# First shift vector of the adaptive modulation summed on VectorE, second shift's products placed between mixer tiles, silu after two of four sums of squares

## The chip, the cores and the metric

The kernel runs on one core of a Trainium2 chip. A core has a matrix engine (TensorE, PE in the profile; its weight loads are PEld), VectorE (DVE), ScalarE (ACT), GpSimd (POOL) and SyncE (SP), which here only issues transfers. The metric is the time of one execution in device microseconds, as the median of several runs; lower is better.

## The reference, cut to what matters

Two blocks run one after the other on x (512 tokens of 1024 channels, f32). The change touches only the start of the first block:

```python
def ada_mods(cond, w, b):                       # c: 1x1024, w: 1024x6144
    mods = (jax.nn.silu(cond) @ w + b)[..., None, :]
    return jnp.split(mods, ADA_CHUNKS, axis=-1) # six vectors of 1024

sh1, sc1, g1, sh2, sc2, g2 = ada_mods(c, ada_w[i], ada_b[i])
u = modulate(rms_norm(x, mix_pre_g[i]), sh1, sc1)   # h * (1 + scale) + shift
y = pool_mixer(u, pool_w[j], pool_scale[j])         # (window mean - u) @ w, 4 groups of 256 channels
x = x + g1 * rms_norm(y, mix_post_g[i])
f = conv_ffn(modulate(rms_norm(x, ffn_pre_g[i]), sh2, sc2), ffn_w_up[i], ...)
x = x + g2 * rms_norm(f, ffn_post_g[i])
```

Behind it come the feed-forward part, a gated delta rule mixer and a gated linear attention mixer, each with large f32 products. They make up the span from about 80 us on and are the same in both kernels.

## The kernel before, in words

All six vectors come from one matrix of 24 MB. It is read in 24 units of 1 MB: unit u = 4j + n holds 256 rows of the 1024 columns of vector j (j = 0 first shift, 1 first scale, 2 gate, 3 second shift, 4 second scale, 5 second gate). SP issues them in this order into six slots in SBUF (tile `ada`), each once its slot is free, and puts between them the two halves of the mixer's weights `pool_w` (0.5 MB each) and the first feed-forward weights `raw` (1 MB). The order of the program text is the order on every engine; counters (semaphores) carry the waits.

For vectors 0 to 4 PE multiplies each unit with silu(c) (`ada_unit`, four products of 512 columns on four groups of 32 array columns, line 1787), and counts it in `ada_used`, which frees the slot. After four units VectorE copies the sums to SBUF (`ada_sum`, line 1099), PE adds the four groups and turns the row into columns (`mod_col`, 32 tiny products, line 1797), and VectorE adds the bias (lines 1106 to 1110). The gate takes `mod_row` instead, the second shift's copy is ScalarE's (line 617). Vector 5 is summed by VectorE much later, with one scalar_tensor_tensor per 128 rows (line 1236).

Meanwhile ScalarE normalises x (squares, line 504, root, line 509, scaling, line 573), PE applies the window means in eight `pool_block`s (line 1823), ScalarE copies their results and scales them by 1 + sc1 (line 581), VectorE adds the shift times the sums of the window (line 1150) and scales `pool_w` (line 1138). PE then multiplies each of four token tiles by the mixer weights (`mixed(0)` to `mixed(3)`, eight products each, line 1838). For each tile ScalarE takes squares and root of y, VectorE adds it to x, ScalarE takes squares and root of the new x and scales it to `xn` (lines 504, 509, 597), and PE turns it (`turn_normed`, line 1757), with the units of vectors 3 and 4 between. On ScalarE these steps stand in a fixed order: y0, y1, u0, y2, u1, y3, then the copy of line 617, then u2 and u3. `keep_busy` (line 1763) is PE work without use.

What sets the order around the change is thus the text itself: SP's list of loads, PE's list of units, blocks and tiles, ScalarE's list of squares and scalings.

## Time and profile before

| what | value |
|---|---|
| median of 3 runs | 1144.46 us (1143.86 to 1144.51) |
| profiled execution | 1143.81 us, span 1142.0 us |
| PE / PEld busy | 1125.4 / 920.0 us |
| DVE / ACT / POOL busy | 542.1 / 505.8 / 451.0 us |
| granted PE clock, mean | 0.997 |
| transfers | 128.97 MB, mean 113 GB/s |
| one unit of the adaptive matrix | 1 MB, median 11.3 us from issue to landing |

A time in a row counts from the span's start. Busy PE time includes pipelining, so it is not PE at its peak; what matters for the change is which wait ends last in the first 83 us, since behind that point the work is the same.

### The profile page before, as it was taken

The page shows a single profiled execution, that of the slowest core. Times are in us where ns is not written, and L with a number is a line of the kernel's source. Part 1 is how long each engine was busy: PE and PEld are TensorE (multiplying, and loading weights), DVE is VectorE, ACT ScalarE, POOL GpSimd, SP SyncE. Part 2 cuts the span into 40 slices and gives each one's busy share as a digit, 9 for nine tenths or more (in the row PEclk, how much of TensorE's full clock was granted, in tenths as well). Part 3 has the DMA queues.
Part 4 walks back from the last instruction along what each step waited for, and adds up shares of the span by engine and source line. Part 5 has one row for each costly group of instructions (what it writes and reads, how often), then busy time and mean ns, then how long its engine had stood idle before and what let it go on. Part 6 is the DMA issues. An engine that isn't in the chain of part 4 may idle for free.

```text
span 1142.0 us, 17109 instructions
## 1 busy us (share of the span) xinstructions
PE 1125.4 (99%) x6818; PEld 920.0 (81%) x6818; DVE 542.1 (47%) x878; ACT 505.8 (44%) x701; POOL 451.0 (39%) x342
## 2 busy tenths in 40 slices
PE   9899999999999999999999999999999999999997
PEld 6568888888888888888788878888888888888886
DVE  2472554324452234567986556422200443676825
ACT  4474453544421223875443255754422343534632
POOL 0015544545455371654432211035354444564430
PEclk9999999999999999999999999999999999999999
DMA  8993232232342333434242211122343322223201
GB/s 342 412 376 125 74 110 83 101 110 73 110 128 78 111 111 112 148 106 116 74 114 72 75 38 38 74 74 74 111 124 109 111 79 93 94 75 111 75 1 74
DMA packets 86216, 128.97 MB, mean 113 GB/s; under 512 B 13300, under 2 KB 66306, under 8 KB 85895
## 3 DMA queue, kind: packets, MB, share of 16 engines
q1 hardware_dynamic: 80706, 119.62, 30.8%
q10 hardware_dynamic: 5445, 8.42, 2.2%
q8 instruction: 48, 0.79, 0.3%
q14 instruction: 17, 0.14, 0.0%
HBM read 122.77 MB, written 5.26 MB: 112 GB/s over the span
## 4 chain that ended last, share of the span: by engine, by line
PE 96%; ACT 2%; DVE 2%; issue 1%; POOL 0%; DVEq 0%; ACTq 0%; POOLq 0%
PE ps L292 26%; PE ps L294 25%; PE ps L293 25%; PE ps L1757 3%; PE ps L1787 1%; PE ps L1838 1%; PE ps L2228 1%; PE ps L2229 1%; PE ps L1763 1%; PE ps L2297 1%; PE ps L2287 1%; PE ps L2234 1%; PE ps L1823 1%; PE ps L2052 1%; PE ps L2414 1%; PE ps L2120 1%
## 5 line engine op out<-in xcount | busy, mean ns | idle before, releaser
L429 POOL TENSOR_TENSOR wl<-raw,wh 128x512 fp32r<-128x512 f32 x312 | 420.4, 1379 | 611.6 <-ACT wh L480 611.6
L292 PE MATMUL ps<-xth,wh 128*128 128x512 f32 (+1 forms) x832 | 324.5, 390 | 1.2 <-DVE xtl L1189 0.9
L294 PE MATMUL ps<-xth,wl 128*128 128x512 f32 (+1 forms) x832 | 317.5, 382 | 0.0
L293 PE MATMUL ps<-xtl,wh 128*128 128x512 f32 (+1 forms) x832 | 317.2, 381 | 0.0
L480 ACT ACTIVATE wh<-raw 128x2048 fp32r<-128x2048 f32 x78 | 149.3, 1914 | 305.0 <-PE ps L294 281.3
L292 PEld LDWEIGHTS ps<-xth,wh 128*128 128x128 f32 x832 | 156.5, 188 | 33.8 <-issue 3.7
L294 PEld LDWEIGHTS ps<-xth,wl 128*128 128x128 f32 x832 | 156.4, 188 | 30.6
L293 PEld LDWEIGHTS ps<-xtl,wh 128*128 128x128 f32 x832 | 156.6, 188 | 28.7 <-issue 0.5
L1197 DVE SCALAR_TENSOR_TENSOR conv_out<-ps,conv_taps,conv_out 128x511 f32<-128x511 f32 x44 | 32.7, 744 | 124.8 <-ACT conv_out L650 124.8
L1292 DVE SCALAR_TENSOR_TENSOR conv_v<-ps,gdn_taps,conv_v 128x511 f32<-128x511 f32 (+2 forms) x96 | 71.8, 748 | 40.3 <-ACT conv_v L718 37.4
L292 PE MATMUL ps<-wh,xth 128*128 128x512 f32 x176 | 69.8, 396 | 0.0
L294 PE MATMUL ps<-wh,xtl 128*128 128x512 f32 x176 | 68.6, 390 | 0.0
L293 PE MATMUL ps<-wl,xth 128*128 128x512 f32 x176 | 68.5, 389 | 0.0
L292 PE MATMUL ps<-wh,act_parts_h 128*128 128x512 f32 x160 | 62.4, 390 | 0.0
L293 PE MATMUL ps<-wl,act_parts_h 128*128 128x512 f32 x160 | 62.3, 389 | 0.0
L294 PE MATMUL ps<-wh,act_parts_l 128*128 128x512 f32 x160 | 62.3, 389 | 0.0
L1596 DVE SCALAR_TENSOR_TENSOR xres<-xres,ps 128x1024 f32<-128x1024 f32 x7 | 8.5, 1220 | 90.9 <-PE ps L294 90.9
L718 ACT ACTIVATE conv_v<-ps,gdn_taps 128x512 f32<-128x512 f32 x32 | 21.8, 683 | 55.7 <-PE ps L294 31.0
L292 PE MATMUL ps<-wh,ogt_h 128*128 128x512 f32 x112 | 43.7, 391 | 0.0
L293 PE MATMUL ps<-wl,ogt_h 128*128 128x512 f32 x112 | 43.6, 389 | 0.0
L294 PE MATMUL ps<-wh,ogt_l 128*128 128x512 f32 x112 | 43.6, 389 | 0.0
L1223 DVE CAST act_parts_h<-acts 128x512 fp32r<-128x512 f32 x20 | 9.9, 495 | 65.3 <-PE ps L294 65.3
(349 smaller groups left out, 1634.1 us busy)
## 6 DMA issues: line engine op xcount, KB each, us to landing
ada<-in_ada_w SPq DMA_DIRECT2D x24, 1024.0 KB, 11.3
raw<-in_gdn_w_in SPq DMA_DIRECT2D x24, 1024.0 KB, 5.3
raw<-in_ffn_w_up SPq DMA_DIRECT2D x22, 1024.0 KB, 4.9
raw<-in_gla_w_in SPq DMA_DIRECT2D x12, 1024.0 KB, 5.1
raw<-in_ffn_w_down SPq DMA_DIRECT2D x11, 1024.0 KB, 4.9
raw<-in_gdn_w_out SPq DMA_DIRECT2D x8, 1024.0 KB, 4.9
raw<-in_gla_w_out SPq DMA_DIRECT2D x4, 1024.0 KB, 5.0
xres<-in_x SPq DMA_DIRECT2D x4, 512.0 KB, 5.1
```

The source lines that it names most:

```text
L292: nc.tensor.matmul(o, lh, rh, start=first, stop=False)
L293: nc.tensor.matmul(o, lh, rl, start=False, stop=False)
L294: return nc.tensor.matmul(o, ll, rh, start=False, stop=last)
L429: rest = nc.gpsimd.tensor_tensor(lo[:, part], raw[:, s, part], hi[:, part].bitcast(f32), ALU.subtract)
L480: nc.scalar.activation(wh[:, s if w is None else w, :], raw[:, s, :], ACT.Copy).then_inc(hi_done, 1)
L718: nc.scalar.activation(conv_v[:, sub, :], ps[:, piece_bank(piece), :], ACT.Copy, scale=gdn_taps[:, 3, ch:ch + 1]).then_inc(S("tap3"), 1)
L1197: V.scalar_tensor_tensor(dst[:, 1:T], src[:, 0:T - 1], conv_taps[:, 0, ds(chunk, 1)], dst[:, 1:T], ALU.mult, ALU.add).then_inc(S("conv_lef ...
L1292: V.scalar_tensor_tensor(dst[:, j:T], src[:, 0:T - j], gdn_taps[:, 3 - j, ch:ch + 1], dst[:, j:T], ALU.mult, ALU.add)\
L1757: return X.transpose(o, x, ident[0:n, 0:n])
L1763: X.matmul(ps[:, b, 0:256], ones[:, 0:1].broadcast_to([P, P]), group_rows[:, 0:1].broadcast_to([P, 256]), start=True, stop=True)
L1787: mm = X.matmul(ps[c:c + 32, j % 2, :], c_col[:, k:k + 1].broadcast_to([P, 32]), ada[:, u % ADA_SLOTS, b, half * 512:half * 512 + 512], st ...
L1823: mm = X.matmul(ps[:, 4 + cb % 4, c0:c0 + nc_], xn[:, tt, cb * P:(cb + 1) * P], band_of(cb // 2, tt), start=(tt == 0), stop=(tt == TT - 1) ...
```

## The change

- SP: units 6 to 9 no longer wait for PE's use of units 0 to 3 but for VectorE's sums over them (`shift_summed`). Units 12 and 13 move behind the first feed-forward weights. All units still wait for the fourth tile of x, whose arrival now has a counter of its own (`x_last`).
- VectorE forms the first shift vector: a multiplication and seven scalar_tensor_tensor instructions over 1024 columns into `shift_acc`, behind the window sums. PE's units 0 to 3 and their 32 tiny products go; eight products of `shift_acc` with a column of ones (`shift_col`) come, behind the first scale.
- VectorE scales the first half of `pool_w` before it finishes the scale's column, and the second half in the middle of the shift additions, as before.
- ScalarE: a silu of four columns of ones (a dummy) loads the table. Two sums of squares come before the silu of c, two behind it. The scaling by 1 + sc1 waits for the scale alone.
- PE: `pool_block`s 0 to 3, unit 4, `pool_block`s 4 to 7, units 5 to 7; four `keep_busy` products before unit 8; unit 12 before `mixed(2)` and unit 13 inside it; units 14 and 15 behind `mixed(3)`.

The counts of the semaphores are moved accordingly.

```diff
+                if u >= ADA_SLOTS + 4:
+                    sp.wait_ge(S("ada_used"), u - ADA_SLOTS - 3)
+                elif u >= ADA_SLOTS:
+                    sp.wait_ge(S("shift_summed"), 2 * (u - ADA_SLOTS) + 2)
...
-            sp.wait_ge(S("x_in"), 16 * TT)
+            sp.wait_ge(S("x_last"), 16)
...
-            for u in range(8, 14):
+            for u in range(8, 12):
                 ada_unit(u)
             unit(0, (0, w_up[0, 0]))
-            for u in range(14, 20):
+            for u in range(12, 20):
                 ada_unit(u)
...
-            act.wait_ge(S("rows_turned"), 1)
-            nc.scalar.activation(c_col[:], ps[:, 6, 0:KD], ACT.Silu).then_inc(S("c_silu"), 1)
+            act.wait_ge(S("prepared"), 11)
+            nc.scalar.activation(glast_exp[:, 0, :], ones[:, 0:TT], ACT.Silu)
             for tt in range(TT):
-                act.wait_ge(S("x_in"), 16 * TT)
+                if tt == TT // 2:
+                    act.wait_ge(S("rows_turned"), 1)
+                    nc.scalar.activation(c_col[:], ps[:, 6, 0:KD], ACT.Silu).then_inc(S("c_silu"), 1)
+                act.wait_ge(S("x_in"), 16 * (TT - 1))
+                if tt == TT - 1:
+                    act.wait_ge(S("x_last"), 16)
                 square_sum(junk[:], xres[:, tt, :], stat[:, 0, tt:tt + 1])
...
-            act.wait_ge(S("mods_done"), 2)
+            act.wait_ge(S("mods_done"), 1)
...
+            def shift_sum(k):
+                u = k // 2
+                if k % 2 == 0:
+                    v.wait_ge(ada_full[u], 16)
+                if k == 0:
+                    V.tensor_scalar(shift_acc[:], ada[:, u, 0, :], c_col[:, 0:1], None, ALU.mult).then_inc(S("shift_summed"), 1)
+                else:
+                    v.wait_ge(S("shift_summed"), k)
+                    V.scalar_tensor_tensor(shift_acc[:], ada[:, u, k % 2, :], c_col[:, k:k + 1], shift_acc[:], ALU.mult, ALU.add)\
+                        .then_inc(S("shift_summed"), 1)
...
-            ada_sum(0)
-            mod_col(0, 2, SH1)
...
+            for k in range(KD):
+                shift_sum(k)
             ada_sum(1)
+            scale_weights(0)
             mod_col(1, 3, SC1, PRE1)
+            mod_col(0, 2, SH1)
...
+            def shift_col(b):
+                pe.wait_ge(S("shift_summed"), KD)
+                for k in range(KD):
+                    mm = X.matmul(ps[:, b, k:k + 1], shift_acc[:, k * P:(k + 1) * P], ones[:, 0:1], start=True, stop=True)
+                mm.then_inc(S("mod_mm"), 1)
...
-            ada_unit(0, 0)
-            ada_unit(0, 1)
...
-            ada_unit(0, 2)
-            ada_unit(0, 3)
+            ada_unit(1, 0)
...
-            mod_col(0, 2, 0)
-            mod_col(0, 2, 1)
-            for n in range(4):
+            for n in range(1, 4):
                 ada_unit(1, n)
             mod_col(1, 3, 0)
             mod_col(1, 3, 1)
+            shift_col(2)
+            pe.wait_ge(S("pooled_done"), KD)
+            keep_busy(4, 7)
             ada_unit(2, 0)
-            pe.wait_ge(S("pooled_done"), KD)
...
             mixed(1, gate_row)
-            mixed(2)
+            ada_unit(3, 0)
+            mixed(2, second_shift)
             mixed(3)
-            for n in range(4):
-                ada_unit(3, n)
+            ada_unit(3, 2)
+            ada_unit(3, 3)
             turn_normed(0)
```

PE between the last `pool_block` and the first mixer tile, in the kernel before. Rows of line 1797 are `mod_col`, of 1787 `ada_unit`:

```order
L1797 MATMUL ps<-group_rows,ada_part 32x1 [waits ada_summed]
L1797 MATMUL ps<-group_rows,ada_part 32x1 x15
L1797 MATMUL ps<-group_rows,ada_part 32x1 [waits ada_summed]
L1797 MATMUL ps<-group_rows,ada_part 32x1 x15
L1787 MATMUL ps<-ada,c_col 32x512 [waits ada_full4]
L1787 MATMUL ps<-ada,c_col 32x512 x3
L1787 MATMUL ps<-ada,c_col 32x512 [waits ada_full5]
```

And from units 6 and 7 on in the changed kernel, whose lines 1806, 1816, 1902 and 1783 are `ada_unit`, `mod_col`, `shift_col` and `keep_busy`:

```order
L1806 MATMUL ps<-ada,c_col 32x512 [waits ada_full1]
L1806 MATMUL ps<-ada,c_col 32x512 x3
L1816 MATMUL ps<-group_rows,ada_part 32x1 [waits ada_summed]
L1816 MATMUL ps<-group_rows,ada_part 32x1 x15
L1816 MATMUL ps<-group_rows,ada_part 32x1 [waits ada_summed]
L1816 MATMUL ps<-group_rows,ada_part 32x1 x15
L1902 MATMUL ps<-ones,shift_acc 128x1 [waits shift_summed]
L1902 MATMUL ps<-ones,shift_acc 128x1 x7
L1783 MATMUL ps<-group_rows,ones 128x256 [waits pooled_done]
L1783 MATMUL ps<-group_rows,ones 128x256 x3
L1806 MATMUL ps<-ada,c_col 32x512 [waits ada_full2]
```

The first set of `mod_col` is gone, and eight full-width products and four of `keep_busy` stand between the scale's column and unit 8.

VectorE over the same stretch, before (line 1086 is the window sums, 1138 the scaling of `pool_w`):

```order
L1086 COPY band_sum<-ps 128x512 [waits pool_mm] x3
L1099 COPY ada_part<-ps 128x512 [waits ada_used]
L1106 TENSOR_TENSOR mod_cols<-ps,cond_cols 128x8 [waits mod_mm]
L1099 COPY ada_part<-ps 128x512 [waits ada_used]
L1108 SCALAR_TENSOR_TENSOR mod_cols<-ps,cond_cols 128x8 [waits mod_mm]
L1110 TENSOR_TENSOR mod_cols<-mod_cols,cond_cols 128x8 [waits cols_done]
L1138 TENSOR_TENSOR pool_w<-pool_w,pool_scale_row 128x1024 [waits pool_in,vec_done,cols_done,mods_done]
```

and now, from the last of the eight shift sums on:

```order
L1098 SCALAR_TENSOR_TENSOR shift_acc<-ada,c_col,shift_acc 128x1024 [waits shift_summed,ada_full3]
L1098 SCALAR_TENSOR_TENSOR shift_acc<-ada,c_col,shift_acc 128x1024 [waits shift_summed]
L1118 COPY ada_part<-ps 128x512 [waits ada_used]
L1155 TENSOR_TENSOR pool_w<-pool_w,pool_scale_row 128x1024 [waits vec_done,pool_in]
L1127 SCALAR_TENSOR_TENSOR mod_cols<-ps,cond_cols 128x8 [waits mod_mm]
L1129 TENSOR_TENSOR mod_cols<-mod_cols,cond_cols 128x8 [waits cols_done]
L1125 TENSOR_TENSOR mod_cols<-ps,cond_cols 128x8 [waits mod_mm]
```

The scaling of `pool_w`, with its wait for the mixer weights, now stands ahead of the scale's column.

## Rows read from the trace of the kernel before

**Rows 1.** The page: busy time, share of the span, instructions.
```profile
PE 1125.4 (99%) x6818; PEld 920.0 (81%) x6818; DVE 542.1 (47%) x878; ACT 505.8 (44%) x701; POOL 451.0 (39%) x342
```
**Rows 2.** Windows: length, busy PE, PEld, DVE, ACT, POOL, granted clock, DMA share, GB/s.
```profile
16.50:18.00 1.50, 1.50 (x8) 1.50 (x8) 0.21 (x1) 1.43 (x3) 0.00 (x0) 0.50 1.04 423
...
63.00:64.50 1.50, 1.50 (x20) 0.52 (x16) 0.43 (x2) 1.47 (x4) 0.00 (x0) 1.00 0.59 90
```
**Rows 3.** Timeline of SP's transfer issues: start, length, count.
```profile
9.60 13.50 SPq L327 DMA_DIRECT2D ada<-in_ada_w  x8
...
23.65 0.69 SPq L337 DMA_DIRECT2D pool_w<-in_pool_w  x1
27.96 9.97 SPq L327 DMA_DIRECT2D ada<-in_ada_w  x6
37.98 0.47 SPq L304 DMA_DIRECT2D raw<-in_ffn_w_up  x1
...
62.82 0.37 SPq L327 DMA_DIRECT2D ada<-in_ada_w  x1
...
63.68 0.37 SPq L327 DMA_DIRECT2D ada<-in_ada_w  x1
```
**Rows 4.** Issue to landing (us): unit 8; pool_w halves; raw; units 18 and 19.
```profile
ada<-in_ada_w SPq DMA_DIRECT2D x1, 1024.0 KB, 10.8
...
pool_w<-in_pool_w SPq DMA_DIRECT2D x2, 512.0 KB, 12.0
...
raw<-in_ffn_w_up SPq DMA_DIRECT2D x1, 1024.0 KB, 16.0
...
ada<-in_ada_w SPq DMA_DIRECT2D x1, 1024.0 KB, 5.3
...
ada<-in_ada_w SPq DMA_DIRECT2D x1, 1024.0 KB, 6.9
```
**Rows 5.** Chain of waits, 22 to 67 us: start, length, what.
```profile
28.76 4.01 PE ps L1823 x32
...
33.40 3.50 PE ps L1787 x31
...
37.66 0.75 PE ps L1797 x58
...
45.32 1.10 PE ps L1838 x4
...
52.27 9.50 PE ps L1838 x44
61.76 3.57 PE ps L1787 x32
...
66.36 0.36 PE ps L1797 x32
```
**Rows 6.** Timeline of VectorE: window sums, pool_w, shift additions, a later sum.
```profile
19.23 2.48 DVE L1086 COPY band_sum<-ps 128x512 f32<-128x512 f32 x4
...
38.84 1.23 DVE L1138 TENSOR_TENSOR pool_w<-pool_w,pool_scale_row 128x1024 f32<-128x1024 f32 x1
...
39.98 2.73 DVE L1150 SCALAR_TENSOR_TENSOR pooled<-band_sum,mod_cols,pooled 128x512 f32<-128x512 f32 x4
...
131.61 5.24 DVE L1236 SCALAR_TENSOR_TENSOR g_acc<-ada,c_col,g_acc 128x1024 f32<-128x1024 f32 x4
```
**Rows 7.** Timeline of ScalarE: squares of x and y2, scaling u1, copy of shift 2.
```profile
13.69 1.06 ACT L504 ACTIVATE junk<-xres 128x1024 f32<-128x1024 f32 x1
...
58.35 1.02 ACT L504 ACTIVATE junk<-ps 128x1024 f32<-128x1024 f32 x1
...
63.84 1.13 ACT L597 ACTIVATE xn<-xres,stat 128x1024 f32<-128x1024 f32 x1
...
65.40 0.60 ACT L617 ACTIVATE ada_part<-ps 128x512 f32<-128x512 f32 x1 [0.43 <-PE ps L1787]
```
**Rows 8.** Timeline of PE: a turned tile; keep_busy at full clock.
```profile
65.27 1.09 PE L1757 MATMUL ps<-ident,xn 128*128 128x128 f32 x8
...
74.19 2.78 PE L1763 MATMUL ps<-group_rows,ones 128*128 128x256 f32 x12
```

More of the change, by code:

```diff
@@ L119, in build @@
     post1_row = at("post1_row", PH + 8 * KB, [D])
+    shift_acc = at("shift_acc", PH + 4 * KB, [D])
     ada_part = at("ada_part", PH + 12 * KB, [2, 512])
@@ L323, in ada_unit @@
             def ada_unit(u):
-                if u >= ADA_SLOTS:
-                    sp.wait_ge(S("ada_used"), u - ADA_SLOTS + 1)
+                if u >= ADA_SLOTS + 4:
+                    sp.wait_ge(S("ada_used"), u - ADA_SLOTS - 3)
+                elif u >= ADA_SLOTS:
+                    sp.wait_ge(S("shift_summed"), 2 * (u - ADA_SLOTS) + 2)
                 sp.dma_start(ada[:, u % ADA_SLOTS], ada_v[u // 4, u % 4]).then_inc(ada_full[u % ADA_SLOTS], 16)
@@ L331, in _ @@
             for tt in range(TT):
-                sp.dma_start(xres[:, tt, :], a["x"][0, tt * P:(tt + 1) * P, :]).then_inc(S("x_in"), 16)
-            sp.wait_ge(S("x_in"), 16 * TT)
+                sp.dma_start(xres[:, tt, :], a["x"][0, tt * P:(tt + 1) * P, :]).then_inc(S("x_in") if tt < TT - 1 else S("x_last"), 16)
+            sp.wait_ge(S("x_last"), 16)
             for u in range(8):
@@ L613, in _ @@
             norm_scale(1)
-            act.wait_ge(S("ada_used"), 16)
+            act.wait_ge(S("ada_used"), 12)
             act.wait_ge(S("mod_mm"), 2)
-            act.wait_ge(S("ada_summed"), 3)
+            act.wait_ge(S("ada_summed"), 2)
             nc.scalar.activation(ada_part[:, 1, :], ps[:, 1, :], ACT.Copy).then_inc(S("ada_summed"), 1)
@@ L1088, in ada_sum @@
             def ada_sum(j):
-                v.wait_ge(S("ada_used"), 4 * j + 4)
+                v.wait_ge(S("ada_used"), 4 * j)
                 if j >= 2:
@@ L1097, in ada_sum @@
                     if j == 4:
-                        v.wait_ge(S("ada_summed"), 4)
+                        v.wait_ge(S("ada_summed"), 3)
                     V.tensor_copy(ada_part[:, j % 2, :], ps[:, j % 2, :]).then_inc(S("ada_summed"), 1)
             def mod_col(j, b, which, gain=None):
-                v.wait_ge(S("mod_mm"), j + 1)
+                v.wait_ge(S("mod_mm"), (2, 1, 3, 4, 5)[j])
                 out, bias = mod_cols[:, which, :], cond_cols[:, which, :]
@@ L1108, in mod_col @@
                     V.scalar_tensor_tensor(out, ps[:, b, 0:KD], 1.0, bias, ALU.add, ALU.add).then_inc(S("cols_done"), 1)
-                    v.wait_ge(S("cols_done"), 9 if which == SC1 else 12)
+                    v.wait_ge(S("cols_done"), 10 if which == SC1 else 12)
                     V.tensor_tensor(out, out, cond_cols[:, gain, :], ALU.mult).then_inc(S("mods_done"), 1)
@@ L1140, in scale_weights @@
                                 .broadcast_to([P, 2, GDIM // P, GDIM]), ALU.mult).then_inc(S("cols_done"), 1)
+            for k in range(KD):
+                shift_sum(k)
             ada_sum(1)
+            scale_weights(0)
             mod_col(1, 3, SC1, PRE1)
+            mod_col(0, 2, SH1)
             v.wait_ge(S("mods_done"), 2)
-            v.wait_ge(S("cols_done"), 8)
             for cb in range(KD):
-                if cb % 4 == 0:
-                    scale_weights(cb // 4)
+                if cb == KD // 2:
+                    scale_weights(1)
                 v.wait_ge(S("pooled_done"), KD + cb + 1)
@@ L1630, in layer_norm @@
                 v.wait_ge(S(name + "_in"), 32)
-                v.wait_ge(S("x_in"), 32 * TT)
+                v.wait_ge(S("x_in"), 16 * (2 * TT - 1))
                 for tt in range(TT):
@@ L1778, in ada_unit @@
                 pe.wait_ge(ada_full[u % ADA_SLOTS], 16 * (u // ADA_SLOTS + 1))
-                if n == 0 and j >= 2:
-                    pe.wait_ge(S("ada_summed"), j - 1)
-                    if j >= 3:
-                        pe.wait_ge(S("mods_done"), 3)
+                if n == 0 and j >= 3:
+                    pe.wait_ge(S("ada_summed"), j - 2)
+                    pe.wait_ge(S("mods_done"), 3)
                 for b in range(2):
@@ L1791, in mod_col @@
             def mod_col(j, b, half):
-                pe.wait_ge(S("ada_summed"), j + 1)
+                pe.wait_ge(S("ada_summed"), j)
                 for k in range(4):
@@ L1802, in mod_row @@
             def mod_row(j, b):
-                pe.wait_ge(S("ada_summed"), j + 1)
+                pe.wait_ge(S("ada_summed"), j)
                 for half in range(2):
@@ L1903, in gate_row, with second_shift @@
                     mod_row(2, 0)
+            def second_shift(g):
+                if g == 1:
+                    ada_unit(3, 1)
             mixed(0, gate_unit)
             mixed(1, gate_row)
-            mixed(2)
+            ada_unit(3, 0)
+            mixed(2, second_shift)
             mixed(3)
-            for n in range(4):
-                ada_unit(3, n)
+            ada_unit(3, 2)
+            ada_unit(3, 3)
             turn_normed(0)
@@ L1948, in _ @@
             pe.wait_ge(S("mods_done"), 5)
-            pe.wait_ge(S("ada_summed"), 5)
+            pe.wait_ge(S("ada_summed"), 4)
             up_units(0)
```

1 line of the change is left out of this document (removed).

## The prediction

> **What bounds the kernel now.** I read the page first: PE is busy 99% of the span [rows 1], so a microsecond is won only where PE's work is shortened or a stall of it goes. Behind 83 us nothing changes; the question is when the first feed-forward product can run. So I read the chain of waits up to there, then the windows, the transfer issues with their landings, and the timelines of the helpers.
>
> The chain [rows 5] shows PE nearly all the way: blocks of window means (32 records in 4.01 us), units of the adaptive matrix (four in 3.50 to 3.57 us, 0.9 us each), the mixer tiles. It leaves PE for VectorE between 38.4 and 45.2 us, where the scale and shift become ready, and comes back at 45.32 for the mixer's third weight group. The second bound does not show in the chain: the transfers. Six units start at 9.60 [rows 3]. Unit 8, tenth in the queue counted in MB, was issued at 27.96 and landed 10.8 us later, at 38.8; `raw`, the sixteenth, at 37.98 + 16.0 = 54.0 [rows 3, 4]. That is 15.2 us for 6 MB, 2.53 us per MB: the queue is full and a transfer's place in it sets its landing, at 38.8 + 2.53 x (place - 10). In one spot it runs dry (90 GB/s at 63 us [rows 2]), because units 18 and 19 wait for slots freed only after the mixer: they are issued at 62.82 and 63.68 and land at 68.1 and 70.6, where a full queue would bring them at 66.6 and 69.1 (places 21 and 22).
>
> **The change, part by part.** The profiled execution took 1143.81 us for a span of 1142.0, so 1.8 us lie around the span; the median shown is 0.65 us above it. I sum changes and add them to the median, 1144.46.
>
> *ScalarE's start.* Two squares, each about 1.2 us with its reading of the sum (1.06 alone [rows 7]), move ahead of the silu into idle time, so x is normalised up to 2.5 us earlier. The cover is PE's window sums (last copy at 19.23 + 2.48 = 21.7 [rows 6]) and then the transfers. Even if PE begins its blocks no earlier than now, at 22.7, it does 4.0 + 0.9 + 4.0 + 1.8 (units 4, 5, 6) and stands at 33.4, while unit 7 (place 8) lands at 33.7. So this edit is worth nothing beyond 0.3 us, and unit 7's landing is the new start of the path. The wait for x keeps its place for the loads: zero. If the cover went, 1 us more would come.
>
> *Shift on VectorE.* Four units (3.6 us) and a `mod_col` (0.75 us) leave PE. VectorE pays eight instructions at 5.24 / 4 = 1.31 us [rows 6], 10.5 us from 21.7: done at 32.2, before it is wanted at 34.6. Units 6 to 9 now wait for the second, fourth, sixth and eighth of them: 24.3, 26.9, 29.6, 32.2. Behind unit 6 on SP stand `pool_w` and all later loads; their data would begin to flow at about 27, 29.5, 34.6 and 37, so the queue stays full and nobody waits. Cost zero; late by 3 us it would start to cost.
>
> *From unit 7 to the mixer's third group.* Unit 7 is done at 33.7 + 0.9 = 34.6, against 33.40 + 3.50 = 36.9 before: 2.3 us earlier, and the scale's `mod_col` ends at 36.1 against 38.4 [rows 5]. From there PE has `shift_col`, `keep_busy`, unit 8, two groups (1.1 each) and unit 9. `keep_busy` is 8 records at 2.78 / 12: 1.85 us [rows 8]. `shift_col` is 16 records (f32 products come as two) that load 128 columns of weights and stream one. No row has that. Below, the whole `mod_col`, 64 records of quarter width, takes 0.75 us [rows 5]; above, `keep_busy` records at 0.23 give 3.7 us. Nearest is a turned tile, full width with short streams, 1.09 / 8 = 0.136 [rows 8]; with less to stream I take 0.12, 1.9 us. So the third group can start at 36.1 + 1.9 + 1.85 + 0.9 + 2.2 + 0.95 = 43.9.
>
> The Trainium skill ("TensorE: Matmul & The Clock Gate", "Back-to-back issue gap") gives about 81 ns for a weight load with a product of 128 columns; that would make `shift_col` an estimated 1.3 us and the start 43.3. The trace's 136 ns for the turned tile is dearer, and the sum keeps to it.
>
> VectorE's side of the same meeting: `pool_w` is issued up to 23.65 and lands 12.0 us later on the mean of its halves, the second near 36.2 [rows 3, 4], its place unchanged. VectorE, which now waits for it ahead of the column, needs 1.23 for the scaling [rows 6] and 0.4 for the column: scale ready at 37.9, against 38.8. ScalarE's first scaling takes 0.65, so the shift additions start at 38.6, against 39.98 [rows 6]: 1.4 us earlier, and the third group's data come at 43.9. Both sides agree; before it was 45.32. **Gain at the mixer: g = 1.4**, less 0.1 for semaphores: 1.3.
>
> *Units 12 and 13 inside the mixer.* They land at 51.5 and 54.0 (places 15 and 16), before PE reaches them (53.5 and 56.2), and SP then issues units 18 and 19 at about 54.5 and 57: the queue no longer runs dry. But tile 2 ends later relative to its start by two units, 3.57 / 2 = 1.8 us. Before it ended at 52.27 + 9.50 x 14/22 = 58.3 (14 of 22 products), and ScalarE took its squares at 58.35 [rows 7] without waiting. Now it ends at 58.3 - 1.3 + 1.8 = 58.8. From there ScalarE goes without a pause through u0, y2, u1, y3 and the scaling of u1, which ended at 63.84 + 1.13 = 65.0 [rows 7] and now ends at 65.5; then the copy of line 617, 0.6, and PE's first half of the second shift's `mod_col` can start at 66.2. It started at 66.36 [rows 5]. PE itself is ready at 65.1 and stands idle for a microsecond: what is late next is ScalarE. **Net: -0.15 us.** In general the start is 67.5 - g, so all of the first 1.15 us of g is spent here. Behind it both kernels do the same; units 18 and 19 are there in time.
>
> Sum: 1144.46 - 0.15 = 1144.3 us. With `shift_col` at its bounds, g is between -0.5 and 1.4 (VectorE's side caps it), the time between 1144.2 and 1146.1.
>
> **Rivals.**
>
> *A. The gain is kept.* If ScalarE catches up (it no longer waits 4 us for `raw`, which moves to place 14 and lands at 48.9), only the transfers bound: unit 19 at 69.1 is used by 70.0 instead of 71.6, so -1.6: 1142.9. For it: the dry spot goes. Against: ScalarE's chain restarts at tile 2's end in any case. No mechanism gives more than these 1.6 us, since the queue starts when it did and its bytes are the same.
>
> *B. PE's new work is dear.* `shift_col` at 3.7 us: g = -0.5, +1.6: 1146.1. For it: f32 weight loads of full width show about 190 ns in the trace's other lines. Against: they are overlapped there.
>
> *C. The clock falls, slower than before.* At 16.5 us the granted clock was 0.50, 1.2 GHz in place of 2.4 [rows 2], behind about 2.5 us of narrow transposes and one-row products. Now PE waits for units 6 and 7 and VectorE's copy, and from 35.3 to 38.0 has only products of one column. If the clock is low from 38 until the third group, 5.9 us of work take twice that: g = 1.3 - 5.9 = -4.6, and 67.5 + 4.6 is 5.7 us later: 1150.1. It costs more than measurement can miss once some 3.5 us of work run at half. Against: before, between 37 and 42, PE was idle in longer pieces and kept the full clock, and `keep_busy` stands there. The skill's same page ("HAM oscillation — how this bites in real kernels") says that waits for transfers between short bursts throw the clock back; by that rule this rival would be the forecast.
>
> *D. The queue starves*, if VectorE's sums begin over 3 us later than 21.7 (a late silu): each microsecond beyond costs one. 1146 or more.
>
> **How the numbers follow.** The forecast 0.48, A 0.20, B 0.20, C 0.08, D 0.04. The likeliest gives 1144.3 us. The range reaches from just below A to just above B: 1142.7 to 1147.0. A measurement of this kernel can tell about 0.2%, 2.3 us, from no change: faster means below 1142.2, which no mechanism reaches, 0.04 for what I overlook; slower means above 1146.8, C and part of B and D, 0.09; the same 0.87.
>
> **What would show it.** Unit 7 lands at 33.7 and PE waits for it. The scaling of `pool_w` at 36.2 waits for its transfer. `shift_col` takes 1.9 us. The third mixer group starts at 43.9; tile 2's squares at 58.8; PE waits for the copy on ScalarE until 66.2; the rate of transfers stays above 400 GB/s from 12 to 69 us. The prediction is wrong if the clock leaves 1.00 behind 20 us, if VectorE's sums end behind 35, or if ScalarE does not hold PE at 65 us.

## The result and the profile after

The changed kernel took 1146.69 us in the median of 20 runs (1145.17 to 1149.89), the kernel before, beside it on the same chip, 1144.57 (1143.58 to 1146.43). The ratio is 1.0018 with an interval of 1.0012 to 1.0024: slower, by 2.1 us. The forecast was 1144.3, no change. Its range, 1142.7 to 1147.0, held the time; its sign and its likeliest case did not, and it had given slower a chance of 0.09.

The execution that was profiled is the shortest of the 20: 1145.17 us, span 1143.3 against 1142.0. The page's busy times, as in [rows 1]:

```profile
PE 1126.7 (99%) x6746; PEld 921.3 (81%) x6746; DVE 552.4 (48%) x885; ACT 505.8 (44%) x702; POOL 450.2 (39%) x342
```

PE has 72 records fewer and is busy 1.3 us longer: its work takes longer in time, not in count. VectorE has the 10 us of the shift sums. The timeline of PE in the changed kernel, from unit 7 to the first feed-forward product (start, length, what, and in brackets the idle time before it and what ended it):

```profile
33.02 1.07 PE L1806 MATMUL ps<-ada,c_col 128*32 128x512 f32 x8 [0.76 <-DMA ada<-in_ada_w]
34.90 0.71 PE L1816 MATMUL ps<-group_rows,ada_part 128*32 128x1 f32 x64 [0.81 <-DVE ada_part L1118]
35.54 1.95 PE L1902 MATMUL ps<-ones,shift_acc 128*128 128x1 f32 x16
37.34 2.66 PE L1783 MATMUL ps<-group_rows,ones 128*128 128x256 f32 x8
39.93 1.94 PE L1806 MATMUL ps<-ada,c_col 128*32 128x512 f32 x8
...
44.76 1.13 PE L1857 MATMUL ps<-pool_w,pooled 128*128 128x256 f32 x4
...
58.17 5.45 PE L1857 MATMUL ps<-pool_w,pooled 128*128 128x256 f32 x24
...
67.29 0.43 PE L1816 MATMUL ps<-group_rows,ada_part 128*32 128x1 f32 x32 [0.79 <-ACT ada_part L624]
...
78.88 0.47 PE L293 MATMUL ps<-xth,wh 128*128 128x512 f32 x1 [0.95 <-DVE xtl L1209]
```

Unit 7 takes 1.07 us and unit 8, the same work, 1.94: the clock. The windows of the changed kernel there (columns as in [rows 2], the clock third from the end):

```profile
36.00:37.50 1.50, 1.50 (x15) 1.50 (x15) 1.15 (x3) 0.28 (x1) 0.00 (x0) 1.00 1.03 423
37.50:39.00 1.50, 1.50 (x7) 1.27 (x8) 1.11 (x3) 1.50 (x3) 0.00 (x0) 0.83 1.05 426
39.00:40.50 1.50, 1.50 (x7) 0.48 (x9) 1.50 (x3) 1.50 (x4) 0.00 (x0) 0.50 1.00 401
40.50:42.00 1.50, 1.50 (x9) 0.20 (x2) 1.50 (x3) 1.50 (x3) 0.00 (x0) 0.53 1.03 418
```

The same stretch of the kernel before has 1.00 all through, although PE was busy for 3.1 us of the six there:

```profile
36.00:37.50 1.50, 0.88 (x10) 0.00 (x0) 0.58 (x1) 0.00 (x0) 0.00 (x0) 1.00 1.04 421
37.50:39.00 1.50, 0.92 (x68) 0.78 (x72) 0.60 (x4) 0.16 (x1) 0.00 (x0) 1.00 1.00 404
39.00:40.50 1.50, 0.85 (x8) 0.00 (x0) 1.50 (x2) 1.50 (x3) 0.00 (x0) 1.00 1.05 429
40.50:42.00 1.50, 0.46 (x2) 0.47 (x3) 1.50 (x4) 1.50 (x4) 0.00 (x0) 1.00 1.02 418
```

The third mixer group starts at 44.76, forecast 43.9, before 45.32 [rows 5]. The second shift's `mod_col` starts at 67.29, forecast 66.2, before 66.36. The first feed-forward product starts at 78.88; in the kernel before this row is:

```profile
77.92 0.47 PE L292 MATMUL ps<-xth,wh 128*128 128x512 f32 x1 [0.95 <-DVE xtl L1189]
```

So 0.96 us are lost by then, and 0.3 more until the end of the span. VectorE's side (changed kernel) went as forecast; it answers to [rows 6]:

```profile
21.16 0.74 DVE L1095 TENSOR_SCALAR shift_acc<-ada,c_col 128x1024 f32<-128x1024 f32 x1
21.93 9.41 DVE L1098 SCALAR_TENSOR_TENSOR shift_acc<-ada,c_col,shift_acc 128x1024 f32<-128x1024 f32 x7
...
35.68 1.23 DVE L1155 TENSOR_TENSOR pool_w<-pool_w,pool_scale_row 128x1024 f32<-128x1024 f32 x1 [0.84 <-DMA pool_w<-in_pool_w]
```

ScalarE's chain, which answers to [rows 7], holds PE before the second shift, as forecast:

```profile
60.20 1.02 ACT L507 ACTIVATE junk<-ps 128x1024 f32<-128x1024 f32 x1 [3.36 <-PE ps L1857]
...
65.62 1.14 ACT L604 ACTIVATE xn<-xres,stat 128x1024 f32<-128x1024 f32 x1
66.66 0.57 ACT L624 ACTIVATE ada_part<-ps 128x512 f32<-128x512 f32 x1
```

And the dry spot of the transfers [rows 2] is gone, without use: 429 GB/s in the changed kernel where 90 stood.

```profile
63.00:64.50 1.50, 1.50 (x15) 0.54 (x17) 1.47 (x2) 1.47 (x5) 0.00 (x0) 1.00 1.04 429
```

### The profile page after: what moved, and what is told of

It reads as the page before. It is cut to its first block, busy times and chain, and to the rows that moved or that the text cites. A ratio compares the mean times of both kernels' runs of the same rounds, so it can differ in the third digit from the quotient of the medians.

```text
span 1143.3 us, 16973 instructions
## 1 busy us (share of the span) xinstructions
PE 1126.7 (99%) x6746; PEld 921.3 (81%) x6746; DVE 552.4 (48%) x885; ACT 505.8 (44%) x702; POOL 450.2 (39%) x342
## 4 chain that ended last, share of the span: by engine, by line
PE 85%; issue 5%; POOL 5%; DVE 3%; ACT 2%; DMA 1%; ACTq 0%; DVEq 0%; POOLq 0%
PE ps L293 23%; PE ps L295 23%; PE ps L294 23%; POOL wl L432 3%; PE ps L1777 3%; PE ps L1783 1%; PE ps L1857 1%; PE ps L1806 1%; PE ps L2258 1%; PE ps L2259 1%; PE ps L2327 1%; POOL attn L456 1%; PE ps L2317 1%; PE ps L2264 1%; PE ps L2444 1%
## 5 line engine op out<-in xcount | busy, mean ns | idle before, releaser
L1217 DVE SCALAR_TENSOR_TENSOR conv_out<-ps,conv_taps,conv_out 128x511 f32<-128x511 f32 x44 | 32.7, 744 | 124.9 <-ACT conv_out L657 124.9
L295 PE MATMUL ps<-wh,ogt_l 128*128 128x512 f32 x112 | 43.6, 389 | 0.0
L294 PE MATMUL ps<-wl,ogt_h 128*128 128x512 f32 x112 | 43.6, 389 | 0.0
```

Of the source, the lines that this page charges most:

```text
L294: nc.tensor.matmul(o, lh, rl, start=False, stop=False)
L295: return nc.tensor.matmul(o, ll, rh, start=False, stop=last)
L1217: V.scalar_tensor_tensor(dst[:, 1:T], src[:, 0:T - 1], conv_taps[:, 0, ds(chunk, 1)], dst[:, 1:T], ALU.mult, ALU.add).then_inc(S("conv_lef ...
```

## The experiments

Each kernel of eleven runs was timed in five rounds beside the kernel before; "before" below is its median there. Edits are against the changed kernel unless said otherwise. The runs were spread over three chips, so a median is compared with its own "before" first. Every profile, that of the kernel before too, also shows half clock in its last 2 to 5 us; "the clock held" below speaks of the stretch from 20 to 1130 us.

**The changed kernel again, five more executions.** First eleven runs with a profile:

> The changed kernel as it is, beside the others. What is asked: which executions are long, and whether their mean granted clock is lower. If the clock makes the loss, times and mean clock go together (about 1145.3 us at 0.996, 1147.3 at 0.994) and the profile shows a stretch at 0.50 between 37 and 42 us. If the placing of units 12 and 13 alone makes it, the times lie close together, near 1145.4 us.

Measured: 1146.22 (before 1144.43), ratio 1.0017 (1.0008 to 1.0026). The slowdown repeats. The times come in groups: of 35 executions in all, 17 took 1145.2 to 1146.3, 14 took 1146.9 to 1148.0, and 4 took 1148.7 to 1149.9, at mean clocks of 0.995 or 0.996, mostly 0.994, and 0.993. Four more profiled executions were to show what parts them:

> The changed kernel once more, for one look at another execution. Theory: where the mean granted clock is 0.994 in place of 0.996 (about half of its executions, 1.7 us longer), there is one more spell of half clock of the same length as that at 38 us, at full price, inside the first 80 us. Rival: the longer executions lose it in the later stages, with the clock at 1.00. If this execution has 0.996 it tells nothing of this but repeats the profile of the changed kernel: one spell at 38 us, steady products at 84.0 to 84.3.

> The changed kernel, another look at one execution. Theory: its time follows from how long the clock is at half between 36 and 46 us: 3.4 us give 1145.2 to 1146.3 and steady products at 84.0 to 84.3, 10.2 us gave 1149.2 and 88.2; an execution at 1147.2 has a length between them and steady products near 86. Rival: steady products at 84 and the rest lost later.

> As for the look before it: the lengths of half clock between 36 and 46 us and the start of the steady products go together, about 2 us later at twice the length of 3.4 us. Rival: the two are independent.

> As for the two looks before it. With six profiled executions of the changed kernel, the theory holds if those over 1146.6 us all begin their steady products later than 85 us and those under it all before 85.

Six profiled executions of the same kernel, by their time (us):

| time | half clock at | third group | second shift's mod_col | first product |
|---|---|---|---|---|
| 1145.17 | 38.5 to 41.9 | 44.76 | 67.29 | 78.88 |
| 1145.22 | 37.9 to 41.3 | 45.02 | 67.56 | 79.14 |
| 1145.56 | 37.7 to 41.1 | 45.27 | 67.81 | 79.40 |
| 1147.08 | 35.4 to 42.3 | 46.54 | 69.08 | 80.66 |
| 1147.08 | 36.8 to 43.6 | 47.03 | 69.56 | 81.15 |
| 1149.19 | 36.0 to 46.3 | 48.89 | 71.44 | 83.03 |

Nearly the whole spread of these six is made before the third group, and it follows how long the clock stays at half: 3.4, 6.8 or 10.2 us. From there every execution needs the same 22.5 us to the `mod_col` and 11.6 more to the product. (The steady products of the expectations begin 5.15 us behind the first: at 84.0 to 84.6, 85.8, 86.3 and 88.2. The three executions over 1146.6 are the three over 85.) The longest one, in its windows and in `shift_col`'s and `keep_busy`'s rows:

```profile
33.00:36.00 3.00, 1.21 (x24) 0.30 (x28) 0.69 (x1) 0.00 (x0) 0.00 (x0) 1.00 1.08 407
36.00:39.00 3.00, 3.00 (x75) 2.98 (x69) 1.47 (x3) 0.84 (x2) 0.00 (x0) 0.50 1.02 420
39.00:42.00 3.00, 3.00 (x11) 2.67 (x11) 1.61 (x4) 3.00 (x6) 0.00 (x0) 0.50 1.02 412
42.00:45.00 3.00, 3.00 (x13) 1.21 (x11) 3.00 (x4) 1.18 (x2) 0.00 (x0) 0.50 1.02 412
```

```profile
36.74 3.57 PE L1902 MATMUL ps<-ones,shift_acc 128*128 128x1 f32 x16
40.18 3.76 PE L1783 MATMUL ps<-group_rows,ones 128*128 128x256 f32 x8
```

Ahead of this fall PE was busy for 1.21 of 3 us (for 2.17 in the shortest execution); in the fall `shift_col`, `keep_busy` and unit 8 all run at half.

**Units 12 and 13 taken back behind the mixer.**

```diff
-            ada_unit(3, 0)
-            mixed(2, second_shift)
+            mixed(2)
             mixed(3)
+            ada_unit(3, 0)
+            ada_unit(3, 1)
```

> The changed kernel with units 12 and 13 back behind mixed(3). Theory (units inside the mixer delay tile 2's squares and with them ScalarE's chain): tile 2's squares start near 57.8 us instead of 60.2, PE reaches the second shift's first tiny products near 65.9 instead of 67.3, and the time falls by 1.2 to 1.5 us against the changed kernel. Rival (only the low clock at 37 to 41 us costs): the squares start earlier, but the time stays within 0.3 us of the changed kernel, and the low stretch is there in both.

Measured: 1145.14 (before 1144.43), ratio 1.0010 (1.0001 to 1.0019). In the profile the clock was at half from 38.6 to 42.0, the third group at 45.31, the second shift's `mod_col` at 66.31, the first product at 77.92, as before. The median is 1.1 us under that of the changed kernel beside it (1146.22), where 1.2 to 1.5 were expected, with half clock in both. With half clock the first part gains nothing; with the units back behind the mixer the fall costs little in this execution.

**The kernel before with units 12 and 13 moved into the mixer, and nothing else.** The same edit the other way round, with `second_shift` as in the change.

> The kernel before with units 12 and 13 alone moved (before and inside mixed(2)). Theory: tile 2's squares move from 58.35 to about 60.7 us (two units and the switching), ScalarE's copy for the second shift to about 67.2, and the kernel is 1.5 to 1.9 us slower than before, at an unchanged clock. Rival (placement free, the clock is all): within 0.3 us of before.

Measured: 1145.52 (before 1144.43), ratio 1.0008 (0.9998 to 1.0017); not told from no change, but the profile is plain. Third group 44.89, `mod_col` 67.40: 22.51 us between them, against 21.04 before. ScalarE's squares of tile 2 start at 60.31, before 58.35 [rows 7]:

```profile
60.31 1.02 ACT L504 ACTIVATE junk<-ps 128x1024 f32<-128x1024 f32 x1 [1.68 <-PE ps L1838]
```

The two units in the mixer cost 1.5 us by themselves; 0.4 of it is hidden here, since this execution reached the third group that much earlier. The median is 1.1 us above before, a little less than the 1.5 to 1.9 expected.

**Fill in PE's waits.**

```diff
             for n in range(1, 4):
+                if n == 3:
+                    keep_busy(2, 2)
                 ada_unit(1, n)
+            keep_busy(2, 2)
             mod_col(1, 3, 0)
```

> The changed kernel with four more keep_busy products where PE waits: two before unit 7, two before the scale's mod_col. Theory (waits between short work let the clock fall): granted clock 1.00 from 20 us on, the mixer's third group at about 44.0 instead of 44.8, the long executions rarer, median 1 to 2 us below the changed kernel. Rival (it is the products of one column, mod_col and shift_col, that count as rest): the clock still falls near 37.7 and the time is the same or 0.3 us longer.

Measured: 1146.02 (before 1144.43), ratio 1.0015 (1.0006 to 1.0024). The profiled execution kept the clock, and it is the forecast come true in every step up to the first product:

```profile
36.00:39.00 3.00, 3.00 (x24) 2.86 (x23) 2.27 (x6) 1.53 (x3) 0.00 (x0) 1.00 1.03 422
39.00:42.00 3.00, 3.00 (x18) 1.67 (x17) 3.00 (x5) 3.00 (x6) 0.00 (x0) 1.00 1.03 412
```

Third group 43.64 (forecast 43.9), squares of tile 2 at 59.06 (58.8), `mod_col` at 66.15 (66.2), first product 77.74, 0.18 earlier than before (forecast 0.15). And yet it took 1145.15 us: 1.6 us went in the gated-delta stage, near 540 us, and 0.2 came back later. Nor did the median follow: it is 0.2 us under the changed kernel's 1146.22, where 1 to 2 were expected. So the fill shows the path of the forecast in one execution and does not win the time back. In that stage VectorE's substitution (products and sums of two operands in SBUF) runs beside a subtraction on GpSimd. The kernel before (VectorE), then this one (VectorE, GpSimd, PE):

```profile
539.82 0.35 DVE L1342 TENSOR_TENSOR diag<-diag,outer 128x184 f32<-128x184 f32 x1
540.21 1.39 DVE L1339 TENSOR_TENSOR outer<-diag 128x198 f32<-128x198 f32 x1
541.63 1.34 DVE L1342 TENSOR_TENSOR diag<-diag,outer 128x198 f32<-128x198 f32 x1
542.89 2.30 DVE L1292 SCALAR_TENSOR_TENSOR conv_v<-ps,gdn_taps,conv_v 128x511 f32<-128x511 f32 x3
```

```profile
540.41 1.32 DVE L1362 TENSOR_TENSOR diag<-diag,outer 128x184 f32<-128x184 f32 x1
541.77 1.34 DVE L1359 TENSOR_TENSOR outer<-diag 128x198 f32<-128x198 f32 x1
543.15 1.33 DVE L1362 TENSOR_TENSOR diag<-diag,outer 128x198 f32<-128x198 f32 x1
544.41 2.30 DVE L1312 SCALAR_TENSOR_TENSOR conv_v<-ps,gdn_taps,conv_v 128x511 f32<-128x511 f32 x3
```

```profile
540.10 5.54 POOL L432 TENSOR_TENSOR wl<-raw,wh 128x512 fp32r<-128x512 f32 x4 [8.42 <-ACT wh L483]
```

```profile
546.86 0.47 PE L293 MATMUL ps<-xth,wh 128*128 128x512 f32 x1 [1.08 <-DVE conv_v L1312]
```

An operation of 0.35 us takes 1.33 while GpSimd works. Three of them instead of two meet it here, the convolution behind them starts 1.5 us later and PE waits 1.08. Which operations meet depends on how the two engines stand to each other, so this loss may come and go with any shift of the front; no run tested that by itself. What the traces show is its place and size: from the first product to the end of the span the 17 other profiles take 0.0 to 1.4 us longer than that of the kernel before, and in all of them a step of 0.2 to 1.3 us stands at one and the same product, which starts at 545.81 in the kernel before. In the profiled execution of the changed kernel the step is 0.4 us, of which 0.2 comes back; the two long operations stand behind the convolution there (544.57 and 545.95), and PE waits for GpSimd's `wl` instead. Since even the kernel before with two units moved has the step, the one profile without it may be the lucky one. The Trainium skill ("SBUF — State Buffer", "🔬 SBUF: two separate sides") says that VectorE and GpSimd share a pair of ports as an exclusive lock, for VectorE operations with two SBUF inputs too; the trace agrees, with 1.33 us for 0.35.

**Fill, and the units behind the mixer.** The fill and the units taken back, together.

> The changed kernel with four keep_busy products (two before unit 7, two before the scale's mod_col) that hold the clock, and with units 12 and 13 behind the mixer as in the kernel before. Theory (the first part gains 1.7 us at the third mixer group once the clock holds, and units between mixer tiles spend it): third group at 43.7 us, no granted clock under 1.00 between 20 and 80 us, tile 2's squares at 56.7, the second shift's mod_col near 64.8, steady products (L293) begin at 81.5 against 83.07 before, and the time is 1143.0 us, or up to 1.2 more if VectorE loses it again between 540 and 560 us where its small products meet GpSimd's subtraction. Rival (the first part brings nothing of itself): steady products at 83 and the time of the kernel before, 1144.4. Rival (executions with a further spell of low clock come whatever fills PE's gaps): the fastest run near 1142.6 but the median near 1144.5.

Measured: 1144.83 (before 1144.73), ratio 0.9998 (0.9989 to 1.0007). The theory missed: this execution's clock fell at 38.4 although PE had hardly been idle. Its windows:

```profile
33.00:36.00 3.00, 2.98 (x79) 1.47 (x77) 0.75 (x2) 0.00 (x0) 0.00 (x0) 1.00 1.07 412
36.00:39.00 3.00, 3.00 (x26) 2.85 (x21) 2.26 (x6) 1.52 (x3) 0.00 (x0) 0.90 1.02 421
39.00:42.00 3.00, 3.00 (x13) 1.22 (x11) 3.00 (x5) 3.00 (x6) 0.00 (x0) 0.53 1.02 410
```

Up to 52 us its program is that of the filled kernel, which held the clock. The same program does either; idle time alone does not decide.

**ScalarE's order around tile 2 turned.** `u0`'s root and scaling and `u1`'s square ahead of the squares of `y2`.

> The changed kernel with ScalarE's order around tile 2 turned: u0's root and scaling and u1's square before the squares of y2, so that ScalarE does them while it would wait for tile 2. Theory (units between the mixer tiles cost because ScalarE's chain restarts only at tile 2's end): y3's squares begin at tile 3's end, 63.7 in place of 64.3, the copy of the second shift at 66.0 in place of 66.66, mod_col at 66.6 in place of 67.3, steady products 0.65 us earlier (83.4), time 1145.9 against 1146.5 of the changed kernel. Rival (PE itself is the bound there): mod_col still at 67.3 and nothing changes. The low clock at 38 us stays in both.

Measured: 1146.79 (before 1144.73), ratio 1.0014 (1.0005 to 1.0023). From the third group (45.21) to `mod_col` (67.51) it takes 22.30 us, in the changed kernel 22.53: 0.23 won where 0.65 was expected. PE still waited 0.57 for the copy: ScalarE's squares of tile 3 now waited 1.05 for PE's end of that tile, and its scaling of tile 1 0.28 for VectorE's statistics. ScalarE's order is a small part of what makes the units dear.

**No keep_busy between shift_col and unit 8.**

> The changed kernel without keep_busy between shift_col and unit 8. Theory (the clock falls because PE waits between 29 and 37.5 us, before keep_busy, which comes too late to prevent it and runs at half clock itself): the clock still falls near 38 us, for as long as with it, and the third mixer group starts 0.5 to 2 us earlier, 42.8 to 44.3, held by VectorE's shift additions; time 1145 to 1146. Rival (keep_busy shortens the spell): without it the low clock lasts beyond 42 us, the third group starts at 45.5 or later and the time is 1147.5 or more.

Measured: 1145.71 (before 1144.73), ratio 1.0009 (1.0000 to 1.0018), third group at 44.70. Half clock all the same, from 39.9 to 43.3, and in this execution from 26.3 to 29.7 too, right behind a wait of 2.46 us for unit 4. PE's groups then wait for VectorE:

```profile
40.32 3.46 PE L1857 MATMUL ps<-pool_w,pooled 128*128 128x256 f32 x8 [0.81 <-DVE pooled L1170]
43.71 1.06 PE L1806 MATMUL ps<-ada,c_col 128*32 128x512 f32 x8
```

`keep_busy` at that place does not protect: the clock falls with it and without it. Whether it costs is open, since the earlier fall brought this execution to `shift_col` 1.0 us later (36.57) than the changed kernel, and it reached the third group at the same time.

**shift_col 64 columns wide.**

```diff
-                    mm = X.matmul(ps[:, b, k:k + 1], shift_acc[:, k * P:(k + 1) * P], ones[:, 0:1], start=True, stop=True)
+                    mm = X.matmul(ps[:, b, 64 * k:64 * k + 64], shift_acc[:, k * P:(k + 1) * P],
+                                  ones[:, 0:1].broadcast_to([P, 64]), start=True, stop=True)
```

VectorE then reads every 64th column of the result.

> The changed kernel with shift_col's products 64 columns wide (the column repeated) in place of one. Theory (it is the run of one-column products, mod_col and shift_col, 2.7 us of them from 35.3 us on, behind which the clock falls): shift_col stays near 1.9 us since its weights set its pace, the granted clock stays 1.00 at 37 to 46 us, the third mixer group starts at 43.7, steady products at 82.9, and the median is 1144.9 with no run above 1146.5. Rival (PE's waits between 31 and 35 us make it fall, whatever shift_col does): half clock near 38 us as in the changed kernel, third group 44.8 or later, median 1146.5 with runs of 1147 to 1149.

Measured: 1145.74 (before 1144.97), ratio 1.0006 (0.9997 to 1.0015). `shift_col` took 2.00 us, as expected. The profiled execution had no fall at 38 but one earlier, from 25.9 to 32.7, that began within a wait of 3.06 us for unit 4: first product at 80.64. Two runs were over 1146.6. The median lies between the two that were expected, and neither theory is borne out.

**Wide and filled, units behind the mixer.**

> Fill in PE's waits (two keep_busy products before unit 7, two before the scale's mod_col), shift_col 64 columns wide, units 12 and 13 behind the mixer. It differs from the filled kernel with the units behind only in the width of shift_col. Theory (narrow products make the clock fall): no low clock between 20 and 1130 us in the profile and in nearly all executions, third group at 43.7, steady products 81.5, median 1143.1. Rival (neither waits nor narrow products, the clock falls with the phase of an execution): half of the executions still lose 1.7 us, median 1144.7 as before.

Measured: 1145.00 (before 1144.97), ratio 0.9999 (0.9990 to 1.0008). All 11 executions had a mean clock of 0.996 or more; with narrow columns 3 of 11 were under that, and 4 of 11 in the first filled kernel. (A mean is a weak sign: it holds the start and the end too, and two profiled executions of the changed kernel have 0.996 with their fall at 38.) In the profile the clock held, the third group stands at 43.96, `mod_col` at 64.94. But the first product came at 77.57, only 0.35 earlier than before, and the time did not move: what is late next is unit 19, for which PE waits 0.84 at 70.25, as its slot is freed behind the mixer again.

**shift_col in PE's wait for unit 7, units behind the mixer.**

```diff
             for n in range(1, 4):
+                if n == 3:
+                    shift_col(2)
                 ada_unit(1, n)
             mod_col(1, 3, 0)
             mod_col(1, 3, 1)
-            shift_col(2)
```

VectorE's waits for the two columns trade places with it.

> The changed kernel with shift_col moved into PE's wait for unit 7 (VectorE's sum is ready at 31.3, unit 7 lands at 33.4), and units 12 and 13 behind the mixer. Theory (a term of 1.9 us leaves the path from unit 7 to the third group, and what stands before it is dense): shift_col at 31.9, unit 7 at 33.8, mod_col at 35.7, keep_busy and unit 8 at 38.8 with its landing, third group at 43.4 to 43.8 if the clock holds, steady products at 81.6 to 82, median 1143.4. Rival (narrow products still stand there, only elsewhere): half clock in 33 to 42 us and third group 44 to 46, median 1144.8 as with the units alone moved back. Rival (PE's waits set it): as the last, with runs of 1147.

Measured: 1143.91 (before 1144.97), ratio 0.9991 (0.9982 to 1.0000), no run over 1145.0. The clock held:

```profile
32.11 1.95 PE L1902 MATMUL ps<-ones,shift_acc 128*128 128x1 f32 x16
33.98 1.06 PE L1806 MATMUL ps<-ada,c_col 128*32 128x512 f32 x8
35.86 0.71 PE L1816 MATMUL ps<-group_rows,ada_part 128*32 128x1 f32 x64 [0.81 <-DVE ada_part L1118]
36.50 2.01 PE L1783 MATMUL ps<-group_rows,ones 128*128 128x256 f32 x8
...
43.97 1.10 PE L1857 MATMUL ps<-pool_w,pooled 128*128 128x256 f32 x4 [0.37 <-DVE pooled L1170]
```

The third group now waits for VectorE's additions, the first product starts at 77.28.

**The same, with shift_col wide and two keep_busy products before the scale's mod_col.**

> shift_col 64 columns wide and in PE's wait for unit 7, two keep_busy products before the scale's mod_col, units 12 and 13 behind the mixer. Theory: PE has full-width work all through 31 to 38 us but for the 0.7 us of mod_col; the clock stays 1.00, the third group starts at 43.5, the second shift's mod_col at 64.8, steady products at 81.5, and the median is 1143.0, faster than the kernel before by 0.1%. Rival: as for the wide and filled kernel, the low clock is a matter of an execution's phase, and the median is 1144.5.

Measured: 1143.72 (before 1144.97), ratio 0.9989 (0.9980 to 0.9998): faster than the kernel before, by 1.25 us by the medians, and 0.3% faster than the changed one by the two ratios (0.9989 / 1.0018). Third group 43.84, `mod_col` 64.81, first product 77.32 and not the 76.4 that 1.5 us at `mod_col` would give: PE waits 0.53 for unit 19 and 0.19 more than before for VectorE, which is 0.7 of the 0.9 missing. All runs lie between 1142.98 and 1145.00.

**The early shift_col alone, units left inside the mixer.**

> The changed kernel with one edit: shift_col stands in PE's wait for unit 7 and no longer behind the scale's mod_col. Units 12 and 13 stay inside the mixer. Theory (1.9 us at the worst place, where they lengthen the path to the third group and go before the fall of the clock, are the larger half of the loss; the units in the mixer the other): third group at 43.9, clock 1.00 from 20 us on, the second shift's mod_col at 66.3, steady products near 83.0, median 1145.0 against 1146.5 of the changed kernel: it ends level with the kernel before. Rival (the early shift helps only with the units behind the mixer): median 1146.0 or more. Rival (the clock falls all the same): half clock between 33 and 46 us in the profile.

Measured: 1145.47 (before 1144.44), ratio 1.0009 (1.0000 to 1.0018). The median is 1.0 us above before, against 1.8 in the changed kernel's eleven runs on another chip: some of the slowdown goes, but the kernel does not end level as expected, and the rival (1146.0 or more) does not fit either. The profile is not as expected. PE came early to unit 4, stood until it landed, and the clock was at half from 26.0 to 29.4:

```profile
26.22 1.93 PE L1806 MATMUL ps<-ada,c_col 128*32 128x512 f32 x8 [2.67 <-DMA ada<-in_ada_w]
```

```profile
24.00:27.00 3.00, 0.78 (x4) 0.20 (x8) 2.86 (x3) 0.19 (x1) 0.00 (x0) 0.84 1.02 412
27.00:30.00 3.00, 3.00 (x18) 1.92 (x11) 1.99 (x2) 0.01 (x1) 0.00 (x0) 0.59 1.01 416
```

Units 5 and 6 end 2.4 us later than in the changed kernel for it, and the third group is at 45.92. The three profiles with a fall at 26 (this one, no `keep_busy`, `shift_col` wide) are those without one ahead of 20 us: where the start runs at full clock, PE does its four blocks early and starves before unit 4. The mean clock of this execution was 0.998, fall included. In the kernel before, units 0 and 1, long landed, stood ahead of the blocks.

## Why the prediction was wrong, point by point

**Right: the start of the path.** Unit 7 landed at 33.0 (forecast 33.7) and PE waited for it. VectorE's sums ended at 31.34 (32.2), seven of its eight instructions at 1.34 us (1.31). The scaling of `pool_w` waited for its transfer at 35.7 (36.2). These moves cost nothing here, as forecast. The cover in front of unit 4 is thin, though: in one of the six profiles of the changed kernel PE waited 1.70 us for it.

**Right: shift_col.** 1.95 us by its row, 1.80 from its start to that of the next (forecast 1.9), and 2.00 with 64 columns: the weights set its pace. The Trainium skill ("TensorE: Matmul & The Clock Gate", "Back-to-back issue gap") led to an estimated 1.3; measured were 1.95 us, 0.122 a record, and the trace sides with the turned tile's 0.136.

**Wrong: the clock, the step that failed.** The sum took every instruction from 38 us on at full speed, and put the fall of the clock, rival C, at 0.08. It fell in all six profiled executions of the changed kernel. The price for 5.9 us of work at half, 5.7 us later and 1150.1, was near: the execution with the longest fall was 5.1 us later and took 1149.19. (The working has such a fall show in the time from some 3.5 us of work at half on. By its own formula 2.5 are enough: 67.5 - (1.3 - 2.5) = 68.7, which is 2.3 us behind 66.36.) What was wrong is its chance, and that it was one case with one price, while the length varies. In the shortest execution it takes 1.1 us of the third group (44.76 against 43.64 with the clock held), in the fifth 3.4, in the sixth 5.3. The argument against it had two halves. "`keep_busy` stands there": it ran at half clock itself, and the clock falls with it and without it. "Before, between 37 and 42, PE was idle in longer pieces and kept the full clock": so it was, in the one profile shown, but that says nothing of the changed kernel, where PE waits for unit 7 and for `ada_part` and has 16 records of one column behind them. That it is these that bring the fall is argued and not shown. The Trainium skill ("TensorE: Matmul & The Clock Gate", "HAM oscillation — how this bites in real kernels") says that waits for transfers between short bursts throw the clock back; by that rule C would have been the forecast, and the traces side with it in part. A wait of 2.67 us was followed by a granted clock of 0.59, and PE busy for 1.21 of 3 us by 9 us at 0.50. But a stretch with 2.98 of 3 us busy was followed by 0.53 as well, and in the kernel before PE was busy for 1.31 of 3 us from 39 to 42 at 1.00 throughout.

**Nearly right: units 12 and 13.** From the third group to `mod_col` the forecast had 66.2 - 43.9 = 22.3 us, the runs have 22.5, and ScalarE holds PE at its end by the chain that was described (0.79 us). Squares at 58.8 were forecast; with the clock held they came at 59.06. The term was 0.2 us short: the stretch of the mixer takes 12.05 us with the two units between its tiles and 9.66 without, so a unit costs 1.2 us there, more than its share of 3.57 / 4. By itself this edit costs 1.5 us of the 21.0 before, and that the forecast had: it set it against a gain of 1.3 that did not come.

**Not seen: what lies behind 83 us.** "Nothing changes" there was wrong by 0.0 to 0.5 us in the six profiles of the changed kernel and by 1.4 in the filled one, with the step at one product near 546 us, where VectorE meets GpSimd.

**The sum.** In the profiled execution, at `mod_col`: forecast -0.15, clock +0.86 (44.76 for 43.9), mixer +0.23, so +0.93. The later stage brings it to +1.3. The median is 1.5 us above that execution, since half of the executions have a mean clock of 0.994 or less and, by the three that were profiled, hold half clock for longer. The median of the kernel before lies 0.8 above its own profiled execution, and 1.3 + 1.5 - 0.8 gives 2.0 of the 2.1 us.

**Rivals.** That the range held the time is luck: its upper end stood there for B, and the time came near it by C. A, B and D fell: no execution of the changed kernel took under 1145.1, the columns were not dear, and 382 to 429 GB/s flowed in every 1.5 us up to 69 us. (The sign "above 400" was too strict: the full queue of the kernel before shows 378 at 31.5 us too.) That A could not be had at this place is now seen too: with the units behind the mixer and the clock held, the landing of unit 19 takes half of the gain; A had named that unit as what would bound it.

**What stays open.** Whether waits, one-column products or neither bring the clock down is not settled: the filled kernel and the filled one with the units behind have the same program up to 52 us, and one kept the clock where the other lost it. Filling the waits and widening the columns together left no execution of 22 under 0.996; filling alone left 7 of 22, widening alone 5 of 11, moving the columns early 3 of 11 with the units behind and 5 of 11 with them inside. These were timed on three chips, and the kernel before itself had 1 of 33, 6 of 27 and 10 of 33 there. Only the first count stands out from all the others, and as a mean of 0.996 does not exclude a fall, it is a hint and no proof. Nor did any edit that keeps the units inside the mixer bring the median back to that of the kernel before: the loss there is shown step by step in single traces, and not undone in a median by holding the clock alone.

## What to carry to other kernels

Where a change makes a tuned start shorter, ask of each stretch that becomes thin (waits for a transfer, products of one column) what the work right behind it costs at half clock, and give that case a length that varies and a chance that is not small; one profile at full clock is no proof of a margin. Small, pace-fixed work such as `shift_col` belongs in a wait that is there anyway: moved there, with the units behind the mixer in both, it went with a ratio of 0.9991 in place of 1.0010, though on another chip. And a gain of a microsecond in front can be lost far behind, where two other engines run close to each other, so read the ends of the stages, not the total alone.

## What the runs showed of the hardware

The times of the changed kernel fall into three groups 1.7 us apart; six profiled executions had one stretch at half clock before the mixer's third group, of 3.4 us in three of the first group, 6.8 in two of the second and 10.2 in one of the third. A product of 128 columns of f32 weights costs 0.122 us a record with one column to stream and 0.125 with 64. A VectorE operation of two SBUF inputs took 1.33 us instead of 0.35 beside GpSimd's subtraction. And `keep_busy` work right behind a thin stretch did not keep the clock: it ran at half itself (3.76 us for 1.96).
